# Forgetting attention's inputs split before the norm's scale is known, and the scale applied where products leave PSUM

## The reference, cut to what matters

```
def rms_norm_2(x, g):
    xf = x.astype(jnp.float32)
    y = xf * lax.rsqrt(jnp.mean(xf * xf, axis=-1, keepdims=True) + EPS)
    return (y * g.astype(jnp.float32)).astype(x.dtype)
...
    x = x + conv_ffn(rms_norm_2(x, ffn_norm[l]), w_up[l], conv_w[l], conv_b[l], w_down[l])
...
            if l == N_A:
                hs = rms_norm_2(x, kv_norm) @ w_kv_shared
                k_sh = hs[..., :MIX_W].reshape(B, S, N_MIX_HEADS, HEAD_DIM)
                v_sh = hs[..., MIX_W:2 * MIX_W].reshape(B, S, N_MIX_HEADS, HEAD_DIM)
                log_f = jax.nn.log_sigmoid(hs[..., 2 * MIX_W:].astype(jnp.float32) + b_fgate.astype(jnp.float32))
                dcum = jnp.cumsum(log_f, axis=1).transpose(0, 2, 1)
            proj = h @ b_w_in[l - N_A]
            q = proj[..., :MIX_W].reshape(B, S, N_MIX_HEADS, HEAD_DIM)
            q_mem = proj[..., MIX_W:].reshape(B, S, N_MEM_HEADS, HEAD_DIM)
            o_mix = forgetting_attention(q, k_sh, v_sh, dcum)
```

## Time and profile before

| | |
|---|---|
| time before, median of 3 runs | 1364.01 us (1361.56 to 1366.23) |
| the profiled execution's own time | 1362.08 us |
| its span | 1360.2 us |
| PE busy | 1153.7 us (85%) |
| weight loads on PE | 1071.4 us (79%) |
| DVE busy | 945.8 us (70%) |
| ACT busy | 697.5 us (51%) |
| POOL busy | 118.2 us (9%) |
| mean granted TensorE clock | 0.912 of full |

### The profile page before, as it was taken

One profiled execution on the slowest core, in us unless ns is written; L12 is line 12 of the kernel. 1 busy time (PEld: TensorE's weight loads), 2 busy tenths in 40 slices (PEclk: granted clock), 3 DMA queues, 4 the chain that ended last, 5 costly groups with the idle time before them and its releaser, 6 DMA issues.

```text
span 1360.2 us, 24905 instructions
## 1 busy us (share of the span) xinstructions
PE 1153.7 (85%) x10397; PEld 1071.4 (79%) x10397; DVE 945.8 (70%) x1723; ACT 697.5 (51%) x1256; POOL 118.2 (9%) x126
## 2 busy tenths in 40 slices
PE   6799866888899669579957799998978859999986
PEld 6688765888788659577945699998977849999886
DVE  5787955667879646676768668877558476778852
ACT  5642256546422465545437656565434464565551
POOL 2000000110000001141000011110011001011100
PEclk9999976989899869889958999998988979999988
DMA  8332111344321005425510145554634303454550
GB/s 337 118 111 77 64 63 32 120 159 148 124 94 66 32 5 191 147 73 195 175 62 1 63 156 183 162 183 161 219 112 159 124 1 127 153 182 162 173 182 31
DMA packets 24448, 167.55 MB, mean 123 GB/s; under 512 B 2704, under 2 KB 2832, under 8 KB 8208
## 3 DMA queue, kind: packets, MB, share of 16 engines
q1 hardware_dynamic: 24336, 165.96, 35.1%
HBM read 164.90 MB, written 1.05 MB: 122 GB/s over the span
## 4 chain that ended last, share of the span: by engine, by line
PE 42%; DVE 35%; ACT 16%; issue 5%; DMA 1%; POOL 1%; POOLq 0%; DVEq 0%; SPq 0%; ACTq 0%
DVE WL L381 8%; PE ps L427 8%; PE ps L422 8%; PE ps L424 8%; DVE ARENA L2033 5%; DVE FR L381 4%; ACT WH L368 4%; PE ps L445 3%; PE ps L453 2%; PE ps L447 2%; ACT ARENA L745 2%; ACT FR L368 2%; PE ps L643 2%; DVE ARENA L2025 2%; ACT L484 2%
## 5 line engine op out<-in xcount | busy, mean ns | idle before, releaser
L381 DVE TENSOR_TENSOR WL<-raw,WH 128x1024 fp32r<-128x1024 f32 (+4 forms) x225 | 262.9, 1191 | 138.0 <-ACT WH L368 137.5
L422 PE MATMUL ps<-FR,WH 128*128 128x256 f32 x1248 | 310.9, 288 | 26.4 <-ACT WH L368 20.4
L424 PE MATMUL ps<-FR,WH 128*128 128x256 f32 x1248 | 307.4, 286 | 1.9 <-POOL FR L501 1.0
L368 ACT ACTIVATE WH<-raw 128x1024 fp32r<-128x1024 f32 (+4 forms) x225 | 217.5, 989 | 111.2 <-PE ps L427 64.4
L422 PEld LDWEIGHTS ps<-FR,WH 128*128 128x128 f32 x1248 | 244.1, 196 | 32.0 <-ACT WH L368 17.8
L424 PEld LDWEIGHTS ps<-FR,WH 128*128 128x128 f32 x1248 | 243.8, 195 | 4.4 <-POOL FR L501 2.1
L422 PE MATMUL ps<-FR,FR 128*128 128x256 f32 x680 | 170.3, 287 | 6.9 <-ACT FR L368 6.3
L427 PE MATMUL ps<-FR,WL 128*128 128x256 f32 x1248 | 170.6, 279 | 0.3 <-DVE WL L381 0.3
L424 PE MATMUL ps<-FR,FR 128*128 128x256 f32 x680 | 169.2, 286 | 0.2 <-DVE FR L493 0.2
L381 DVE TENSOR_TENSOR FR<-raw,FR 128x1024 fp32r<-128x1024 f32 (+2 forms) x100 | 117.2, 1193 | 73.5 <-ACT FR L368 73.5
L427 PEld LDWEIGHTS ps<-FR,WL 128*128 128x128 f32 x1248 | 156.6, 190 | 0.6 <-DVE WL L381 0.6
(11 more groups left out here) (309 smaller groups left out, 1789.7 us busy)
## 6 DMA issues: line engine op xcount, KB each, us to landing
raw<-wst_in SPq DMA_DIRECT2D x124, 1024.0 KB, 5.0
raw<-wst_in SPq DMA_DIRECT2D x14, 768.0 KB, 4.3
raw<-wst_in SPq DMA_DIRECT2D x11, 896.0 KB, 4.8
raw<-wst_in SPq DMA_DIRECT2D x4, 968.0 KB, 4.7
raw<-wst_in SPq DMA_DIRECT2D x2, 912.0 KB, 4.6
cst<-cst_in SPq DMA_DIRECT2D x1, 1681.0 KB, 15.3
X<-xT_in SPq DMA_DIRECT2D x2, 512.0 KB, 6.4
ARENA<-memT_in SPq DMA_DIRECT2D x1, 1024.0 KB, 4.8
```

What stands on the lines that cost most here:

```text
L368: a.activation(hi[:, 0:cols], src, ACT.Copy).then_inc(*put("split_hi", ("hi", i)))
L381: v.tensor_tensor(lo[:, 0:cols], src, hi[:, 0:cols].bitcast(F32), SUB).then_inc(*put("split_lo", ("lo", i)))
L422: pe.matmul(out, hv[:, k, :], src.hi[:, c, :], start=k0 == 0 and k == ks[0], stop=False)
L424: pe.matmul(out, hv[:, k, :], src.lo[:, c, :], start=False, stop=False)
```

## The change

It makes this transition like the other one. `fox_hi` and `fox_lo` are called after each pair of chunks of the down-projection of layer 0: ACT rounds x times `kv_norm` and x times `attn_norm` for both chunks (four operations), DVE makes the four lo parts. They go to two regions of the arena that are free then: `om[0].H` (call it HK) and a new one below it, `HX`. `scaled_v`, `scaled_a` and `scaled_g` are no longer called in the `fox` functions, and POOL has nothing to do there. `mean_mm` moves behind the first item of k. rs (`m.rs`) is multiplied in by DVE at the evictions of the forget gate, k and q; q's eviction moves from ACT to DVE. v has tokens on the partitions, so PE transposes rs once (`rT fox`), DVE copies two columns of it, and both evictions of v multiply by that column. The forget gate's eviction becomes two operations. The jobs' softmax buffers move with the freed memory.

```diff
+    def fox_lo(v, q, l, c0):
+        if l == 0:
+            q.wait_ge(*own("ffn_v"))
+            for to, g, parts in zip(*FOX_IN, (om[0].H, HX[0])):
+                for c in (c0, c0 + 1):
+                    part_x_lo(v, q, parts, to, c, vcol(*g, 0, 8))
+
+    def fox_hi(a, l, c0):
+        if l == 0:
+            for to, g, parts in zip(*FOX_IN, (om[0].H, HX[0])):
+                for c in (c0, c0 + 1):
+                    part_x_hi(a, parts, to, c, vcol(*g, 0, 8))
...
@@ ffn_v, the pairs 4 and 6
             x = X[:, c0:c0 + 2, :]
             v.tensor_tensor(x, x, two(ps), ADD).then_inc(*put("ffn_v", ("x f", l, c0), free))
+            fox_lo(v, q, l, c0)
@@ ffn_a
             q.wait_ge(*got("x f", l, c0))
+            fox_hi(a, l, c0)
             if c0 == 6:
                 q.wait_ge(*got("summed", ("f", l), 2))
@@ fox_pe
-        mean_mm(("f", 0), fm[0].sq[0])
         ps = begin_bank("forget")
...
+                if (c0, i) == (0, 0):
+                    mean_mm(("f", 0), fm[0].sq[0])
+        ps = begin_bank("rT fox")
+        qpe.wait_ge(*got("rstd", ("f", 0)))
+        for b in range(2):
+            ins = pe.transpose(ps[:, 128 * b:128 * b + 128], m.rs[:, 128 * b:128 * b + 128], ident)
+        ins.then_inc(*put("proj", ("rT fox",)))
@@ fox_v
         split_lo(v, q, "forget")
-        rstd_v(v, q, ("f", 0), None, m.q[:, 0, :])
-        scaled_v(v, q, X, vcol("kv_norm_2", None, 0, 8), m.HK, "HK", m.hs, None, mean_bank[:, 0:S])
+        split_lo(v, q, "k pe", 0)
+        rstd_v(v, q, ("f", 0), m.rs, m.y0)
...
-        v.tensor_scalar(d[0], ps[0:12, 0:256], vcol("fgate", None)[0:12, :], None, ADD).then_inc(*put("cmp_v", ("d in",), free))
+        v.tensor_tensor(d[0], ps[0:12, 0:256], m.rs[0:12, :], MUL).then_inc(*put("cmp_v", free))
+        q.wait_ge(*own("cmp_v"))
+        v.tensor_scalar(d[0], d[0], vcol("fgate", None)[0:12, :], None, ADD).then_inc(*put("cmp_v", ("d in",)))
...
-            v.tensor_copy(m.k[:, c0:c0 + 2, :], two(ps)).then_inc(*put("proj_v", ("k", c0), free))
+            v.tensor_tensor(m.k[:, c0:c0 + 2, :], two(ps), bc(m.rs, 1, 2), MUL).then_inc(*put("proj_v", ("k", c0), free))
...
-        scaled_v(v, q, X, vcol("attn_norm_2", 1, 0, 8), m.H, "HX", m.hs, ("f", 0), mean_bank[:, 0:S])
+        ps, free = psum("rT fox")
+        q.wait_ge(*got("rT fox"))
+        v.tensor_copy(m.rT, ps[:, 0:256].rearrange("p (b n) -> p b n", b=2)[:, :, 0]).then_inc(*put("proj_v", ("rT fox v",), free))
...
         for c0 in range(0, 8, 2):
             split_lo(v, q, "q pe", c0)
+            ps, free = psum("q", c0)
+            q.wait_ge(*got("q pe", c0))
+            v.scalar_tensor_tensor(m.q[:, c0:c0 + 2, :], two(ps), 0.125 if c0 < 6 else 1.0, bc(m.rs, 1, 2), MUL, MUL).then_inc(*put("proj_v", ("q", c0), free))
@@ fox_a
-        rstd_a(a, q, ("f", 0), m.q[:, 0, :])
-        scaled_a(a, q, m.HK, "HK", m.hs)
+        rstd_a(a, q, ("f", 0), m.y0)
...
-        scaled_a(a, q, m.H, "HX", m.hs)
...
-            ps, free = psum("q", c0)
-            q.wait_ge(*got("q pe", c0))
-            a.activation(m.q[:, c0:c0 + 2, :], two(ps), ACT.Copy, scale=0.125 if c0 < 6 else 1.0).then_inc(*put("proj_a", ("q", c0), free))
@@ fox_g
-        scaled_g(g_, q, m.HK, "HK", m.hs)
-        scaled_g(g_, q, m.H, "HX", m.hs)
```

More of the change, by code:

```diff
@@ L1992, in __init__ @@
             self.sq = three_squares(m)
+            self.end = m.at
     fm = [FMap() for _ in range(2)]
@@ L2013, in ffn_pe @@
         B.mark("PE", "end", ("F", l), "PE")
+    FOX_IN = ("HK", "HX"), (("kv_norm_2", None), ("attn_norm_2", 1))
+    def fox_lo(v, q, l, c0):
[9 more added lines that the diff above has]
+                    part_x_hi(a, parts, to, c, vcol(*g, 0, 8))
+    HX = [Map(TOP2 - 4 * KC * S).parts(KC)]
     def ffn_v(v, q, l):
@@ L2469, in __init__ @@
             self.Y = m.parts(KC)
-            free = m.at
-            self.H, self.HK = m.parts(KC), m.parts(KC)
-            self.hs = m.some(5, S)
+            self.HK, top = om[0].H, Map(TOP2 - 4 * KC * S)
+            assert fm[0].end <= top.at
+            self.H = HX[0]
+            free = Map(TOP2 - 4 * KC * S)
+            self.y0, self.rs = m(S), m(S)
+            self.rT = m(8)[:, 0:2]
             self.q = m(8 * S, "p (c t) -> p c t", c=8)
@@ L2478, in __init__ @@
             self.MK = m(12 * 384, "p (h n) -> p h n", h=12)
-            assert m.at <= TOP2, m.at
-            at = Map(free)
+            assert m.at <= free.at, m.at
+            at = free
             fox = [self.job(b, par, c0) for b in (1, 0) for c0 in (0, 2, 4) for par in range(2)]
@@ L2561, in fox_v @@
         v.tensor_scalar(d[2], d[1], -1.0, None, MUL).then_inc(*put("cmp_v", ("-d",)))
-        q.wait_ge(*got("lo", "HK", 6))
-        q.wait_ge(*got("lo", "HK", 7))
-        scaled_v(v, q, X, vcol("attn_norm_2", 1, 0, 8), m.H, "HX", m.hs, ("f", 0), mean_bank[:, 0:S])
+        ps, free = psum("rT fox")
+        q.wait_ge(*got("rT fox"))
+        v.tensor_copy(m.rT, ps[:, 0:256].rearrange("p (b n) -> p b n", b=2)[:, :, 0]).then_inc(*put("proj_v", ("rT fox v",), free))
+        q.wait_ge(*own("proj_v"))
         for g in range(2):
@@ L2568, in fox_v @@
             q.wait_ge(*got("v pe", g))
-            v.tensor_copy(m.v[:, 1, 384 * g:384 * g + 384], ps[:, 0:384]).then_inc(*put("proj_v", ("v", g, 1), free))
+            v.tensor_scalar(m.v[:, 1, 384 * g:384 * g + 384], ps[:, 0:384], m.rT[:, 1:2], None, MUL).then_inc(*put("proj_v", ("v", g, 1), free))
         ps, free = psum("dT")
@@ L2605, in fox_a @@
             ps, free = psum("v", g, 0)
+            q.wait_ge(*got("rT fox v"))
             q.wait_ge(*got("v pe", g))
-            a.activation(m.v[:, 0, 384 * g:384 * g + 384], ps[:, 0:384], ACT.Copy).then_inc(*put("proj_a", ("v", g, 0), free))
+            a.activation(m.v[:, 0, 384 * g:384 * g + 384], ps[:, 0:384], ACT.Copy, scale=m.rT[:, 0:1]).then_inc(*put("proj_a", ("v", g, 0), free))
         for c0 in range(0, 8, 2):
             split_hi(a, q, "q pe", c0)
-            ps, free = psum("q", c0)
-            q.wait_ge(*got("q pe", c0))
-            a.activation(m.q[:, c0:c0 + 2, :], two(ps), ACT.Copy, scale=0.125 if c0 < 6 else 1.0).then_inc(*put("proj_a", ("q", c0), free))
         for x, s in m.steps("A"):
```

## The result

The changed kernel took 1345.29 us (median of 4 runs, 1339.79 to 1349.20) beside 1363.70 us of the kernel before in the same comparison: a ratio of 0.9864, 95% interval 0.9841 to 0.9888. Forecast were 1350.2 us and faster. The direction and the range held; the gain was 18.4 us where 13.8 were forecast.

A forecast was written before the change was run, and what follows sets the result against it. PE was taken as the bound through the down-projection, with time won only at its waits or half clock. 10.0 − 0.6 + 2.7 + 1.8 − 0.1 = 13.8 us gain, forecasting 1350.2 us; eight-in-ten range 1343 to 1356.

The forecast's parts named there:

- The end of the down-projection: Last down matmul to k's second item: forecast 7.5 us instead of 17.5, a gain of 10.0 us.
- The model transition: Layer 1's output projection into the up-projection, already in the changed form; its timings priced the end of layer 0's down-projection.
- the slower matmul behind the mean: At k's second item: the first matmul after the mean was expected to cost some 0.2 us extra.
- The cover of 1.6 us: Slack at the mean: due 6.6 us after the last down matmul, POOL's sum expected at 5.0.
- Work beside the down-projection at nothing: Sixteen hi on ACT and sixteen lo on DVE during the down-projection: cost zero, covered by the splits' lead of some 8.
- rival 3: Down-projection: added hi and lo make PE stop once per pair; 11.8 us slower, about 1376; chance 0.02.
- rs: After the mean: rs ready within 15 us of the down-projection's end, needed at 21; cost zero, cover 6 us.
- v without the second scaling: v's sixth item: its split comes on time by some 3 us, PE's wait disappears; gain 2.7 us.
- Rival 2: v's sixth split still late through queue order, wait and mask gaps stay; gain 9.3, time 1354.7 us; chance 0.13.
- The masks: Twelve mask products before q: without waits, five at 0.49 and seven at 0.90, 8.9 us instead of 10.7; gain 1.8.
- Rival 1: Masks and q's first item: clock stays up throughout; 5.4 us more, gain 19.2, time 1344.8 us; chance 0.12.
- q's evictions: q's evictions on DVE take 0.67 against ACT's 0.60; only the last precedes the attention: loss 0.1 us.

## Why the prediction held, and where it was off

**The end of the down-projection: right.** Forecast 7.5 us to k's second item and a gain of 10.0; measured 7.2 and 10.3. The model transition carried every term. The forget gate's item, with its two waits, took 3.88 us from its first matmul to k's (995.81 to 999.69; forecast 3.9), k's first item 2.83 (2.7), the mean 0.67 (0.7). The 0.2 that I had added for the slower matmul behind the mean came too, but not in this stretch, which ends where that matmul starts: the next one starts 0.31 us behind it (1003.19 to 1003.50), elsewhere 0.12. By its own rows the sum should have been 7.3. The cover of 1.6 us that I gave the mean was not used up: POOL's sum (999.28 + 1.30) ended at 1000.6, the mean ran at 1002.5.

**Work beside the down-projection at nothing: right for this kernel, with a wrong reason behind it.** PE had no wait within the down-projection in any of the thirteen traces. But I had counted a lead of some 8 us, let rival 3 decide "only from a delay of 8 us per pair", and had each pair cost PE its delay. The runs with extra work lost 2.3 and 5.8 us at the transition already from delays of 6.0 and 6.9 us per pair on DVE, and not pair by pair but once, at the end, where the last add to x stands in DVE's program behind a split whose tile is late. The lead of the splits over PE was not the right cover to count; the add's place behind the last split was.

**rs: right.** Its last operation ended at 1008.85, 12.9 us after the last down matmul (forecast within 15), and the transposes at 1017.46 did not wait. They cost 0.13 us from start to start, forecast 0.6: the price taken from the attention was too high. Of the 0.4 us lost between k's second item and v, 0.2 is the slower matmul behind the mean.

**v without the second scaling: right.** The copy starts at 1024.56, the splits behind it at 1024.73, and v's wait is gone. The run with HK alone puts it back at 3.44 us, the one with HX alone is without it. Rival 2 did not occur.

**The masks: the term that was mis-sized.** I wrote "I let it fall at the same mask as before and count five products at 0.49 and seven at 0.90". Eleven came at full clock, 4.83 us for them (1034.57 to 1039.40), and one at half: 5.65 us, a gain of 4.9 instead of 1.8. The term was wrong in two ways. Its prices were too high: from start to start a mask takes 0.43 us at full clock and 0.85 at half, where I had divided lengths that include the end of the last product. And the rows of before give the point of the fall as 2.6 us after the first mask (1042.87 to 1045.4); with a gap, that is ahead of the fifth mask, without one it is six masks. Six at 0.43 and six at 0.85 make 7.7 us, 1.1 less than the 8.8 that I had for them. The other 2.0 us of the miss are the fall's point. That the clock falls though the masks have no gaps was right, and shown by the doubled masks; the point at which it falls was not the same, and it is not fixed. Worked out from the stretches' granted clock, with no gap among the masks, it came 5.0, 4.6 and 5.0 us after the first mask in the three profiles of the changed kernel and 5.2 in the doubled one, but 2.4 with the mean first and 2.8 and 2.9 in the two with extra work; the twelve masks took 5.6 to 6.0 us in the changed kernel, 7.7 to 8.2 with the early fall. Each of those other kernels has one profile, so whether their code or the execution makes the fall early is not shown. I had one profile of before, took its point of the fall for the kernel's, and gave full clock a case of its own and nothing between the two. That q's first item came out at 5.3 us as forecast was luck in part: in the third profile it took 4.2. The rest of the distance between 13.8 and the measured 18.4 is within what the medians of four runs leave open: the interval of the ratio gives 15.3 to 21.7 us.

**Rival 1, half true.** Masks at nearly full clock with q's first item at half came out as a mixture that I had not listed. Its full form, clock 1.00 all the way, is what spreading the masks gives, at 30.4 us from the first mask to the attention. The Trainium skill ("TensorE: Matmul & The Clock Gate", the part on the HAM clock gate) ties the clock to how busy PE has been. The doubled masks, 7.70 us busy of 7.70 at a granted clock of 0.50, do not agree with that, with busy time as the profile counts it. What else the gate goes by these runs do not tell; no run varies the number of rows, so that it is the twelve rows which let the clock fall is not shown either.

**q's evictions: right** within what can be seen: the wait ahead of the attention is 0.78 us, before 0.69.

## To carry to other kernels

When a norm's scale waits for the whole input, split input times weight early and multiply the scale in at the evictions; but give PE an item or two that need no scale ahead of the mean, or most of the gain at the transition stays away. Work laid beside a busy stage is free only until it delays the operation that ends this stage, so look at what stands ahead of that one operation in its engine's program, and not at the lead of the stage as a whole. Small products under which the clock falls are better spread among large ones than put in a row (6 us on the kernel before; on the changed kernel likely, not settled), and a term that depends on the clock should be given as a range from several executions.

## What the hardware did that I had not expected

- The granted clock fell to 0.50 under twelve-row products with PE busy all the time (7.70 of 7.70 us), and stayed at 1.00 when the same products came three at a time between q's items.
- The point of the fall varied from 2.4 to 5.2 us after the first mask among kernels whose masks are the same and without a gap. With identical code it came after 5.0, 4.6 and 5.0 us, and the half clock lasted 6.8, 6.8 and 3.4 us, so that q's first item took 5.3, 5.3 and 4.2. From the first mask to the attention this makes 30.45 us in one and 31.95 in the other, with identical code.
- A 12-row product took 0.43 us at full clock and 0.85 at half (starts in the doubled kernel: 1031.40 to 1031.83, 1037.92 to 1038.77), so it scales with the clock in full.
- Code ahead of the change differed by 4.7 us between two profiled executions (941.60 and 946.34 at the down-projection's start), a third of the forecast gain. Spans of two kernels are therefore compared by stretch.
- A DVE operation of 128x256 on two operands in SBUF took 0.94 to 0.96 us in six of sixteen cases, each while POOL was making a lo part, and 0.47 to 0.49 in the others. With one of the two in PSUM it took at most 0.48 beside the same POOL work.
